# Start of a decoder trunk's first layer: order of the loads, squares on ScalarE, column sums inside the second weight tile, and products of zeros at the very start

## What is computed

```python
def rms_norm(x, g, eps=1e-6):
    xf = x.astype(jnp.float32)
    y = xf * lax.rsqrt(jnp.mean(xf * xf, axis=-1, keepdims=True) + eps)
    return (y * g.astype(jnp.float32)).astype(x.dtype)

for i in range(DEPTH):                       # 4 layers
    h = rms_norm(x, norm_g[i])
    y = mixer[i % 3](h, ...)                 # h @ w_in first, @ w_out last
    x = x + y
```

## Time and profile before

| | |
|---|---|
| median of 3 runs | 1822.09 us (1820.61 to 1824.07) |
| the profiled execution | 1820.88 us, span 1819.1 us |
| granted TensorE clock, mean | 0.998 |
| TensorE busy (matmul) | 1767.8 us, 97% |
| VectorE, ScalarE, GpSimd busy | 851.8, 824.9, 550.3 us |

### The profile page before, as it was taken

How to read it: one execution, slowest core, us unless ns; L and a number is a source line. 1 busy time by engine, 2 the same in 40 slices (tenths; PEclk the granted TensorE clock), 3 DMA queues, 4 the chain that set the end, 5 groups by cost and what they waited for, 6 DMA issues and landing times.

```text
span 1819.1 us, 22598 instructions
## 1 busy us (share of the span) xinstructions
PE 1767.8 (97%) x8872; PEld 1431.8 (79%) x8872; DVE 851.8 (47%) x1294; ACT 824.9 (45%) x1191; POOL 550.3 (30%) x143
## 2 busy tenths in 40 slices
PE   7999999999999999999999999999999999999999
PEld 5688789878898666668878888888877887887787
DVE  6765954242142555544643444441277577434410
ACT  6575343685233666644422222222266734338721
POOL 1333320333424000024344444444334234104443
PEclk9999999999999999999999999999999999999999
DMA  4223210222222010112223222222222132012222
GB/s 171 93 70 93 77 39 17 78 93 93 93 93 93 24 47 27 44 47 96 90 94 104 101 92 92 92 98 96 96 84 81 69 102 74 12 47 93 92 94 69
DMA packets 48775, 143.69 MB, mean 79 GB/s; under 512 B 28080, under 2 KB 30256, under 8 KB 32816
## 3 DMA queue, kind: packets, MB, share of 16 engines
q1 hardware_dynamic: 48688, 142.50, 22.9%
HBM read 137.25 MB, written 5.24 MB: 78 GB/s over the span
## 4 chain that ended last, share of the span: by engine, by line
PE 71%; issue 17%; POOL 4%; DVE 4%; ACT 4%; DMA 0%; POOLq 0%; SPq 0%; DVEq 0%; ACTq 0%
PE ps L1565 18%; PE ps L1567 18%; PE ps L1566 18%; POOL w_lo L441 4%; PE ps L1828 2%; PE ps L1884 2%; PE ps L1855 1%; PE ps L2030 1%; PE ps L1870 1%; PE ps L1879 1%; PE ps L2045 1%; PE ps L1839 1%; PE ps L2003 1%; ACT w_hi L531 1%; PE ps L1950 1%
## 5 line engine op out<-in xcount | busy, mean ns | idle before, releaser
L441 POOL TENSOR_TENSOR w_lo<-w_raw,w_hi 128x2048 fp32r<-128x2048 f32 x107 | 497.2, 4646 | 1054.1 <-ACT w_hi L531 842.1
L1565 PE MATMUL ps<-h_hi,w_hi 128*128 128x512 f32 x1488 | 604.3, 406 | 21.8 <-DVE w_lo L959 10.0
L1567 PE MATMUL ps<-h_hi,w_lo 128*128 128x512 f32 x1488 | 581.7, 391 | 0.0
L1566 PE MATMUL ps<-h_lo,w_hi 128*128 128x512 f32 x1488 | 581.3, 391 | 0.0
L1565 PEld LDWEIGHTS ps<-h_hi,w_hi 128*128 128x128 f32 x1488 | 280.4, 188 | 105.0 <-issue 28.9
L1566 PEld LDWEIGHTS ps<-h_lo,w_hi 128*128 128x128 f32 x1488 | 280.6, 189 | 59.5 <-issue 5.5
L1567 PEld LDWEIGHTS ps<-h_hi,w_lo 128*128 128x128 f32 x1488 | 280.2, 188 | 59.6
L531 ACT ACTIVATE w_hi<-w_raw 128x2048 fp32r<-128x2048 f32 (+1 forms) x126 | 238.7, 1894 | 129.1 <-PE ps L1567 123.8
L1565 PE MATMUL ps<-y_hi,w_hi 128*128 128x512 f32 x448 | 174.3, 389 | 0.0
L1566 PE MATMUL ps<-y_lo,w_hi 128*128 128x512 f32 x448 | 174.3, 389 | 0.0
L1567 PE MATMUL ps<-y_hi,w_lo 128*128 128x512 f32 x448 | 174.3, 389 | 0.0
(11 more groups left out here) (190 smaller groups left out, 2285.7 us busy)
## 6 DMA issues: line engine op xcount, KB each, us to landing
w_raw<-w_tiles SPq DMA_DIRECT2D x124, 1024.0 KB, 4.9
x<-x_t SPq DMA_DIRECT2D x4, 512.0 KB, 6.8
out_t<-x SPq DMA_DIRECT2D x8, 256.0 KB, 5.7
w_raw<-w_tiles SPq DMA_DIRECT2D x2, 512.0 KB, 5.0
scr_u<-lt SPq DMA_DIRECT2D x8, 128.0 KB, 2.7
u_blk<-scr_u SPq DMA_DIRECT2D x2, 512.0 KB, 3.3
scr_v<-v_blk SPq DMA_DIRECT2D x2, 512.0 KB, 2.6
scr_t<-v_t SPq DMA_DIRECT2D x2, 512.0 KB, 3.6
```

The lines of the kernel that those rows point to most:

```text
L441: pool.tensor_tensor(w_lo[:, slot, :], w_raw[:, slot, :], w_hi[:, slot, :].bitcast(F32), ALU.subtract).then_inc(lo_done, 1)
L1565: pe.matmul(out_, w_h, m_h, start=start, stop=False)
L1566: pe.matmul(out_, w_h, m_l, start=False, stop=False)
L1567: return pe.matmul(out_, w_l, m_h, start=False, stop=stop)
```

## The change

The loads: x comes in five pieces instead of four, blocks 0 and 1 each by itself. Tile 1 is loaded before both tables instead of between them.

ScalarE: it squares all 8 blocks. Only block 0 is squared early. Blocks 1 and 2 follow after all 8 `round_x`, then `hi(1)` (the rounding of tile 1), then squares 3 to 7.

VectorE: it squares nothing. Its two additions of pairs become four: blocks 1 and 2 onto block 0 ahead of `low_w(1)`, block 4 onto 3 and block 6 onto 5 behind it.

TensorE: four products with ones instead of six, and they stand in tile 1 behind step k == 2 instead of in and behind tile 0. Ahead of all work stand five fp32 products of a zeroed buffer (`rows`, 128 x 512), which wait for its memset alone; their result, in bank 6, is not used.

```diff
+X_LOADS = ((0, 1), (1, 2), (2, 4), (4, 6), (6, 8))
+WARM = 5
...
-        for m in range(KD // 2):
-            sp.dma_start(x[:, 2 * m:2 * m + 2, :], x_in[:, 2 * m:2 * m + 2, :]).then_inc(x_loaded[m], 16)
-            if m == 0:
+        for n, (m0, m1) in enumerate(X_LOADS):
+            sp.dma_start(x[:, m0:m1, :], x_in[:, m0:m1, :]).then_inc(x_loaded[n], 16)
+            if n == 0:
                 sp.dma_start(w_part(w_raw, 0), ...).then_inc(raw[0], 16)
+        sp.dma_start(w_raw[:, 1, :], tiles[1]).then_inc(raw[1], 16)
         sp.dma_start(cf[:, :], const_f).then_inc(loaded, 16)
-        sp.dma_start(w_raw[:, 1, :], tiles[1]).then_inc(raw[1], 16)
         sp.dma_start(cb[:, :], const_b).then_inc(loaded, 16)
...
         def norm(l):                          # ScalarE
             t0 = tile_base[l]
-            hi(t0 + 1)
+            if l:
+                hi(t0 + 1)
...
+        def square_first(m):
+            act.activation(sq8[:, m, :], x[:, m, :], ACT.Square).then_inc(sq0_done, 1)
         for m in range(KD):
-            act.wait_ge(x_loaded[m // 2], 16)
+            act.wait_ge(x_loaded[x_load(m)], 16)
             round_x(0, m)
-            if m % 2 == 0:
-                act.activation(sq8[:, m, :], x[:, m, :], ACT.Square).then_inc(sq0_even, 1)
             if m == 0:
+                square_first(0)
                 hi(0)
+        square_first(1)
+        square_first(2)
+        hi(1)
+        for m in range(3, KD):
+            square_first(m)
...
-            if m % 2:                         # VectorE
-                dve.tensor_tensor(sq8[:, m, :], x[:, m, :], x[:, m, :], ALU.mult).then_inc(sq0_odd, 1)
-            if m in (1, 3):
-                dve.wait_ge(sq0_even, m // 2 + 1)
-                dve.wait_ge(sq0_odd, m // 2 + 1)
-                dve.tensor_tensor(sq8[:, m - 1, :], sq8[:, m - 1, :], sq8[:, m, :], ALU.add).then_inc(sq0_pair, 1)
+        def add_first(to, m):
+            dve.wait_ge(sq0_done, m + 1)
+            dve.tensor_tensor(sq8[:, to, :], sq8[:, to, :], sq8[:, m, :], ALU.add).then_inc(sq0_added, 1)
+        add_first(0, 1)
+        dve.wait_ge(sq0_added, 1)
+        add_first(0, 2)
         low_w(1)
+        add_first(3, 4)
+        add_first(5, 6)
...
+        def sum_first():                      # TensorE
+            pe.wait_ge(loaded, 32)
+            pe.wait_ge(sq0_done, KD)
+            for n, m in enumerate((0, 3, 5, 7)):
+                pe.wait_ge(sq0_added, (2, 3, 4, 4)[n])
+                mm = pe.matmul(ps[7][:, :], ones, sq8[:, m, :], start=(m == 0), stop=(m == KD - 1))
+            mm.then_inc(ss_done, 1)
...
-                if l == 0 and k >= 4:         # first_tiles, tile 0
-                    sum_first((0, 2, 4, 5)[k - 4])
...
-            if l == 0:
-                for m in (6, 7):
-                    sum_first(m)
             ready(t0 + 1)
             for k in range(KD):
...
+                if k == 2 and l == 0:         # first_tiles, tile 1
+                    sum_first()
...
+        pe.wait_ge(zeroed, 1)
+        for _ in range(WARM):
+            pe.matmul(ps[6][:, :], rows[:, 0:P], rows[:, :], start=True, stop=True)
```

More of the change, by code:

```diff
@@ L74, in y_at, with x_load @@
     return (c + 8) % 16
+X_LOADS = ((0, 1), (1, 2), (2, 4), (4, 6), (6, 8))
+def x_load(m):
+    return next(n for n, (m0, m1) in enumerate(X_LOADS) if m0 <= m < m1)
+WARM = 5
 PHASE1 = 10
@@ L304, in trunk @@
     par_loaded, loaded = sem("params_loaded"), sem("const_loaded")
-    x_loaded = [sem(f"x_loaded{m}") for m in range(KD // 2)]
+    x_loaded = [sem(f"x_loaded{m}") for m in range(1 + KD // 2)]
     raw = [sem("raw0_loaded"), sem("raw1_loaded")]
@@ L310, in trunk @@
     sq_done, sum_done = sem("x_sq_done"), sem("x_sum_done")
-    sq0_even, sq0_odd = sem("first_sq_act"), sem("first_sq_dve")
-    sq0_pair = sem("first_sq_pair")
+    sq0_done = sem("first_sq_done")
+    sq0_added = sem("first_sq_added")
     ss_done = sem("x_ss_done")
@@ L1544, in _ @@
         for m in range(KD):
-            dve.wait_ge(x_loaded[m // 2], 16)
+            dve.wait_ge(x_loaded[x_load(m)], 16)
             low_x(0, m)
@@ L1594, in sum_x @@
             pe.matmul(ps[7][:, :], ones, sq[:, (KD - 1) % 2, :], start=False, stop=True).then_inc(ss_done, 1)
[L1596 to L1606, removed]
+        def sum_first():
[5 more added lines that the diff above has]
+            mm.then_inc(ss_done, 1)
         def in_part(t, c, k, start, stop):
```

## The result

The changed kernel takes 1826.63 us (median of 19 runs, 1822.94 to 1829.65), the kernel before 1821.06 us (19 runs, 1819.84 to 1824.07): ratio 1.0028, 95% interval 1.0022 to 1.0034. It is slower, by 5.1 us if the ratio is put on the kernel before. The forecast was 1826.5 us, slower by 4.4.

The account below looks back on a forecast made before the run. The chain from last product with ones to tile 3, 22.5 us, was taken as the bound, not TensorE. Place +2.4, clock +2.0, zeros 0 and tile 3 0 gave +4.4 on 1822.09: 1826.5 us, range 1823.0 to 1829.5.

Parts of the forecast that it names:

- What bounds: Early stretch: the chain from the last product with ones to tile 3, 22.5 us, sets the time, not TensorE.
- B: Rival view at tiles 1 to 3: TensorE's own order sets the end; faster by 1.3 us at most, chance 0.06.
- The place of the sums, +2.4: Products with ones inside tile 1: they end at 26.1 instead of 23.65, so the rstd chain starts 2.4 us later.
- The clock at tile 1, +2.0: After a 3.4 us wait, tile 1's first nine to eleven products run at half clock, ahead of the sums: +2.0 us.
- Rival 1: At tile 1 the clock stays high, so only +2.4 us, 1824.5 us; chance 0.19.
- Zeros, 0: Zero products ahead of tile 0: their gain, up to 2.3 us, goes into idle time before tile 1; counted 0.
- Tile 2 and tile 3: TensorE waits 1.3 us at tile 2, about 3 at tile 3; a slow start there, +1.7, is absorbed, counted 0.
- Rival 3: From 60 to 260 us, later waits totalling 4.6 us take up the delay: 1822 us, no slower; chance 0.10.
- The loads, 0.8 us earlier: With the tables loaded behind it, tile 1 lands 0.8 us earlier, at 14.0 instead of 14.8.
- The sum: All terms together at tile 3, carried to the kernel's end: +4.4 us, 1826.5 us.

Follow-up runs that it names:

- sums_ahead: Changed kernel with its four products with ones moved back between tile 0 and tile 1; 1823.63 us, ratio 1.0008 to the kernel before.
- place_alone: Kernel before with only its six products with ones moved behind step k == 2 of tile 1; 1830.20 us, ratio 1.0045.
- no_zeros: Changed kernel without the five products of zeros; 1825.88 us, ratio 1.0026 to the kernel before.
- early2: Changed kernel, no arithmetic on GpSimd: squares 4 and 5 on VectorE, the others ScalarE, five products with ones ahead of tile 1; 1818.74 us, ratio 0.9988.
- early3: As early2, but with x loaded in four pairs of blocks; 1818.39 us, ratio 0.9984 to the kernel before.
- fill1: Changed kernel with four more products of zeros between tile 0 and tile 1; 1825.28 us, ratio 1.0023 to the kernel before.
- pairs: Changed kernel with x loaded in four pairs of blocks again; 1826.14 us, ratio 1.0023 to the kernel before.
- early: Changed kernel with squares 2, 3 and two additions on GpSimd, squares 6, 7 on VectorE, GpSimd-set ones, sums ahead of tile 1; 1822.03 us, ratio 1.0000.
- fill3: Changed kernel with unused filler products: four between tiles 0 and 1, one ahead of tile 2, three behind it; 1825.66 us, ratio 1.0024.
- sums_k0: Changed kernel with the products with ones behind step k == 0 of tile 1 instead of k == 2; 1823.51 us, ratio 1.0013.

## Why the prediction was right

**What bounds.** Right, and shown: last sum to tile 3 is 22.5 us in every profile, as the prediction read it from the earlier trace rows. B falls with sums_ahead (tile 1 6.0 us later than after, tile 3 2.6 us earlier) and with place_alone (+7.3 at tile 3, where B had +3.0). What the 22.5 us consist of was not taken apart; no run changed anything in them.

**The place of the sums, +2.4.** Right. 3.6 us for four products: 3.59. Tile 1's first product 18.3: 18.28. The last sum at full clock would be at 27.43 less the 1.2 us of the next term, 26.2; the prediction had 26.1.

**The clock at tile 1, +2.0.** Right in kind, too large: six rows at 0.43 instead of nine to eleven, 6 x 0.2 = 1.2 us. Rival 1, the clock stays high, is out for the profiled execution, though the clock did not fall for all of the other versions: in place_alone, tile 1 started fast behind 1.82 us.

**Zeros, 0.** Right. They take 7.63 us, tile 0 is fast and over by 15.0, and the gain goes into the 3.24 us ahead of tile 1. No_zeros agrees. Where the sums directly follow tile 0 (early2, early3) the wait that hides a slow tile 0 is gone and the zeros may be worth something; that was not tried by itself.

**Tile 2 and tile 3.** Waits 1.3 and about 3 us: 1.43 and 3.10. Tile 3's slow start didn't come in the profiled execution after. It did in the four others in which TensorE waited 3.1 us there: place_alone (seven slow rows), fill1 (eight), no_zeros and pairs (twelve each). In place_alone the wait at 198.15 stands at 205.45, +7.3 like tile 3, and in fill1 at 202.76, +4.6 like tile 3: absorbed, as the prediction had it. In no_zeros it stands at 204.29, +6.1 against +5.3 at tile 3, and in pairs at 204.07, +5.9 against +5.0: 0.9 us stayed in both, within the 0 to 1.5 given. So the 0 in the sum is right for the profiled execution and for two of the others, and 0.9 us too low for no_zeros and pairs.

**Rival 3, the later waits take it up.** Out: +3.78 at 201.93 and +3.77 at 583.95.

**The loads, 0.8 us earlier.** Held in the profiled execution (rounding at 13.98, predicted 14.0) and hardly on average: 14.7 over the eleven kernels with the new order. What failed here is the use of two landings of one execution as a rate for all; on average it makes the sum 0.7 us too small, and the clock term makes it 0.8 too large. That the two nearly cancel is luck too. The core's loads from 4 to 8 us move 325 to 394 GB/s in the profile before and about 300 after.

**The sum.** At tile 3, +4.4 predicted and +3.8 measured. The median came out at 1826.63, 0.1 from the forecast, and part of that is luck: on 19 runs the kernel before is 1.0 us faster than on the three that the forecast started from, and the change costs 5.1 us by the ratio, not 4.4. The sum ended at tile 3 and had no term for what comes later. The mean granted clock of the changed kernel over its runs is lower (0.9959 against 0.9985), in part from drops far behind the change, as at 584 and 800 us. They come at a few places and not in every execution: of the 14 profiles, four have the slow rows at 584 (after, no_zeros, pairs, early) and eleven those at 912 that the kernel before has too. Whether and why a shift of 3.8 us makes such drops more frequent stays open; fill3, in which the mean clock is back, leaves +4.3 us between the means (1825.37 against 1821.11).

## What to carry to other kernels

An engine that is 97% busy need not be what bounds a stretch. Find the product whose result the other engines wait longest for, here a few sums that make a norm, and issue it as soon as its inputs are there; filling idle time with it behind other work moves everything after it. Before another engine is given work "for free", ask what it shares with the engines on the path: here GpSimd's squares made VectorE's rows twice as long.

## What the runs showed of the hardware

- The clock fell behind waits of 3.24 us (after, tile 1), 2.64 (no_zeros, tile 1), 2.48 (pairs, tile 1) and 3.11 (place_alone, tile 3), and did not behind 3.10 (after, tile 3), 2.77 (pairs, tile 0) or 1.82 (place_alone, tile 1). In sums_k0 three rows were still fast behind 3.30 us and only then slow. The length of a wait alone doesn't decide.
- A fast start by zeros is not safe: in fill1 rows of tile 0 are slow again from 11.55 on; TensorE had waited 1.96 us between the zeros and tile 0 and started that tile fast at 9.23.
- The column of the granted clock reads 1.00 at the slow start of before (10.0 to 14.6) although the rows are 0.43 us apart. The distance between rows shows the slow start, the column does not.
- GpSimd beside VectorE: 128 x 512 with two SBUF inputs takes VectorE 1.34 to 1.53 us instead of 0.68 to 0.75, and GpSimd 1.5 to 1.6 us; GpSimd's `w_lo`, four times as large, takes 4.64 us on average, 1.16 for such a part.
